# A two-block transformer kernel: the buffers of the split weights start at 0x00 instead of 0xC0 of each 256 bytes

## The chip, the cores and the metric

The kernel runs on one core of one Trainium2 chip. The metric is the device time of one execution in microseconds. It was taken three times for the kernel before; the median is quoted, and one further execution was recorded by the hardware profiler.

## The reference, cut to what matters

The reference is a stack of three kinds of layer on 512 latent rows of width 1024 (and 256 context rows): an FNet layer with a gated feed-forward (`swiglu`), a differential-attention layer with another `swiglu`, and then a hybrid layer (a Mamba-2 scan beside forgetting attention). Nearly all its arithmetic is dense products of activations with weight matrices that are used once:

```
x = x + g2 * swiglu(modulate(rms_norm(x, gain), sh2, sc2), ffn_w_in[i], ffn_w_out[i])   # i = 0 (lat and ctx), i = 1 (lat)
q, k, v = split(h @ diff_w_in, 3);   o = finish(attention(q, k, v)) @ diff_w_out
proj = rmsnorm(h) @ w_in_2           # z, x, B, C, dt, z_att, q, k, v, f, gates
merged = g_ssd * (y_ssd @ w_proj_ssd) + g_att * (y_att @ w_proj_att)
out = h + rmsnorm(merged @ w_out, norm_post)
```

Everything is float32. The kernel keeps that precision by splitting each float32 operand `a` into a rounded part `aH` and a remainder `aL`, both of type float32r, and by forming `a*w` as `aH*wH + aL*wH + aH*wL`.

## The kernel before, in words

**The stream.** SyncE loads the weights in blocks of 128 partitions x 8 x 256 floats (1 MB) in the order of `stream_plan` into a ring of two slots (`ring`, line 240). ScalarE copies a block into `wH` (lines 1833 and 1842) when TensorE has finished with the block two places earlier in the plan. VectorE writes `wL = ring - wH` (lines 2567 and 2578). TensorE then uses the block. `wH` and `wL` have two slots each (`NS = 2`), so one block is split while the other is used. The order of the blocks is written out by hand in `stream_plan`; nothing in it depends on an address.

**How a block is used.** In most products the 128x128 piece of `wH` or `wL` is the stationary operand, loaded by a weight load of its own, and the activations are the moving operand. In four places the activations are stationary and 256 columns of the weight block move: values of the attention (line 1053), the gate rows `z` of the scan (line 1352), the values of the second attention (line 1528) and the last product (line 1299). The helpers `tile` and `exact` (lines 689 and 694) do both feed-forwards. `gemm` (line 1287), `scan_unit` (lines 1333, 1352 and 1356), `narrow` (lines 1503 to 1547), `pair_gemm` (lines 1012 to 1035), `first_pair` (line 1064), `out_part` (line 1115) and `first_unit` (line 950) do the rest.

**Addresses.** `sb` hands out SBUF one buffer behind another, rounded up to 32 bytes, and `phase`/`leave` free what was handed out in a stage. `apart` makes the pair H and L. Empty buffers named `space...` move what follows. With the sizes in the code, the buffers that TensorE reads begin at these addresses modulo 256 (both of a pair alike, and all 128x128 pieces of `w`, all rows of `h1`, `hid`, `un`, `h2` and so on too, because their pitches are multiples of 256 bytes):

| buffer | start modulo 256 | where TensorE starts to read |
|---|---|---|
| `w` | 0xC0 | 0xC0 |
| `h1`, `hid` | 0xC0 | 512 latent columns at 0xC0, 256 context columns at 0x80 (`H1_CTX = LAT + 48`) |
| `h2`, `ao`, `mg` | 0x00 | 0x00 |
| `un` | 0xC0 | 512 columns from column 16: 0x00; the first 272 columns: 0xC0; the last 256: 0x00; as stationary operand 0x00 |
| `ys`, `ya` | 0xC0 | 0xC0 |
| `xs`, `df` (the Fourier transform over rows) | 0x40 | 0x40 |

**Counts.** From the loops, products with a float32r operand pair come in these numbers. Of 512 moving columns at 0xC0 with a piece of `w` stationary: in the feed-forwards 2 layers x 21 units x 48 = 2016 and 2 layers x 24 x 22 = 1056 at line 689 and 96 at line 950, `ys` 384, `ya` 192, together 3744. Of 512 moving columns at 0x00: 576 at line 1547, 192 at line 1287, 192 at line 1115, 144 each at lines 1023 and 1035, 96 at line 1064, together 1344. Of 256 moving columns at 0x80: 1536 at line 694. Of 256 at 0x00: 552 at line 1356, 192 at line 1510, 144 at line 1012, 48 at line 1064, together 936. Of 272 at 0xC0: 552 at line 1356 and 192 at line 1503, together 744. With 256 columns of `w` moving at 0xC0 and 128 stationary columns at 0x00: 768 at line 1352, 576 at line 1053, 384 each at lines 1299 and 1528, together 2112.

Of the kernel before, what the change touches and what calls it, by code (L numbers as in the profile page):

```python
# [12 lines left out]
P = 128  # L13
# [155 lines left out]
def bass_two_blocks_kernel(nc, io, kt_d, dl_d, dc_d, xsave, out):  # L169
# [36 lines left out]
    with ExitStack() as ctx:  # L206
        here = [ctx]

        def sb(name, shape, dt=F32):
            return here[-1].enter_context(nc.sbuf_tensor(name, shape, dt))  # L210
# [31 lines left out]
        def apart(name, shape):  # L242

            return sb(name + "H", shape, F32R), sb(name + "L", shape, F32R)


        def phase():
            s = ExitStack()
            here.append(s)
            return s  # L250

        def leave():
            here.pop().close()

        phase()
        early = sb("early", [P, 4, KC, 256])
        leave()
        wH, wL = apart("w", [P, NS, KC, 256])
        phase()
        xT = sb("xT", [P, KC, ROWS])  # L260
        adacc = sb("adacc", [P, 2, 2, 256])
        condz = sb("condz", [P, KC, 32])
# [51 lines left out]
        yold, xds, zA, gab = gap[:, 0, :], gap[:, 1, :], gap, gap  # L314
        ckT, cqT = sb("ckT", [16, ALL]), sb("cqT", [16, LAT])
        stt4 = sb("stt4", [P, 8])
        sb("space2", [P, 40])
        un = [t[:, :, 0:ALL] for t in apart("un", [P, KC, UN_PITCH])]
        phase()
        zrow = sb("zrow", [P, 4, 512])  # L320
# [56 lines left out]
        leave()  # L377
        leave()
        phase()
        under = sb("under", [P, 6168])  # L380
        orow = sb("orow", [P, 4, D])
        xback = sb("xback", [P, KC, LAT])
        oss, opre, ors = sb("oss", [P, 4, NT]), sb("opre", [P, NT]), sb("ors", [P, NT])
# [3033 lines left out]
```

## Time and profile before

| what | value |
|---|---|
| time, median of 3 runs | 2429.04 us |
| lowest, highest run | 2428.79 us, 2433.89 us |
| the profiled execution: its own time | 2427.2 us |
| the profiled execution: span from first to last instruction | 2425.0 us |
| mean granted TensorE clock | 0.999 |
| instructions | 34386 |

All durations that are used below come from the one profiled execution. Its own time is 2.2 us over its span, and 1.8 us under the median of the three runs. A matmul's duration in the profile is a modelled one: from its start to the moment at which its last column has left the array, so that consecutive matmuls overlap. What a matmul costs a busy TensorE is the distance from its start to the next start.

### The profile page before, as it was taken

How to read it: one execution, taken by the hardware profiler on the slowest of the kernel's cores; microseconds unless marked ns; L12 is line 12 of the kernel's file. 1: busy time of each engine (PE TensorE's matmuls, PEld its weight loads, DVE VectorE, ACT ScalarE, POOL GpSimd, SP SyncE). 2: the span in 40 equal slices, each digit the busy share in tenths (PEclk: the TensorE clock that was granted, in tenths of full speed). 3: DMA queues.
4: the chain of work that ended last, by engine and by line, in shares of the span. 5: the costliest groups of instructions: out<-in, count | busy, mean ns of one | idle time of the engine just before them, and what ended most of it. 6: DMA issues, size and time to landing. Idle time of an engine off the chain costs nothing.

```text
span 2425.0 us, 34386 instructions
## 1 busy us (share of the span) xinstructions
PE 2356.3 (97%) x14108; PEld 1975.3 (81%) x14108; DVE 1367.6 (56%) x2269; ACT 879.5 (36%) x1499; POOL 374.4 (15%) x301
## 2 busy tenths in 40 slices
PE   7899999999999999999999999999999999999999
PEld 5678888888878777657888887988989878887788
DVE  3775766666546767775333336365566445555433
ACT  4332111211234544444222224464545334444432
POOL 0210000000015434501000001143343410000000
PEclk9999999999999999999999999999999999999999
DMA  9834344344321111112333323212222122112223
GB/s 320 218 102 123 122 125 123 121 136 119 94 83 35 36 53 36 36 52 70 104 87 104 90 89 100 71 53 70 70 70 70 53 78 62 54 58 65 85 90 113
DMA packets 252743, 220.76 MB, mean 91 GB/s; under 512 B 7480, under 2 KB 243443, under 8 KB 252204
## 3 DMA queue, kind: packets, MB, share of 16 engines
q1 hardware_dynamic: 249072, 217.92, 29.5%
q8 instruction: 112, 1.84, 0.3%
q10 hardware_dynamic: 3260, 0.58, 0.1%
q14 instruction: 43, 0.35, 0.0%
q0 software_dynamic: 256, 0.07, 0.0%
HBM read 214.26 MB, written 6.29 MB: 91 GB/s over the span
## 4 chain that ended last, share of the span: by engine, by line
PE 60%; DVE 3%; ACT 2%; issue 1%; POOL 1%; DMA 0%; SPq 0%; DVEq 0%; ACTq 0%; POOLq 0%
PE two L689 11%; PE bank L1547 5%; PE bank L1356 5%; PE bank L689 4%; PE bank L1352 3%; PE bank L1333 3%; PE two L1287 3%; PE bank L1053 2%; PE bank L1528 2%; PE two L1567 2%; PE bank L1184 2%; PE two L1158 2%; PE bank L1023 1%; PE bank L1035 1%; PE two L1445 1%
## 5 line engine op out<-in xcount | busy, mean ns | idle before, releaser
L2578 DVE TENSOR_TENSOR wL<-ring,wH 128x512 fp32r<-128x512 f32 x224 | 180.1, 820 | 144.4 <-ACT wH L1842 144.2
L1833 ACT ACTIVATE wH<-ring 128x2048 fp32r<-128x2048 f32 (+1 forms) x80 | 149.2, 1865 | 260.7 <-PE bank L694 69.6
L2567 DVE TENSOR_TENSOR wL<-ring,wH 128x2048 fp32r<-128x2048 f32 (+1 forms) x80 | 180.0, 2250 | 80.1 <-ACT wH L1833 79.9
L689 PE MATMUL two<-h1H,wH 128*128 128x512 f32 x496 | 194.9, 393 | 0.0
L689 PE MATMUL two<-h1H,wL 128*128 128x512 f32 x496 | 193.1, 389 | 0.0
L689 PE MATMUL two<-h1L,wH 128*128 128x512 f32 x496 | 192.9, 389 | 0.0
L1842 ACT ACTIVATE wH<-ring 128x512 fp32r<-128x512 f32 x224 | 133.7, 623 | 57.6 <-PE bank L1333 20.5
L2482 DVE SCALAR_TENSOR_TENSOR adacc<-ring,cond,adacc 128x256 f32<-128x256 f32 x378 | 151.9, 479 | 0.0
L1912 ACT ACTIVATE gateS<-two 128x512 f32<-128x512 f32 x44 | 26.3, 598 | 316.9 <-PE bank L694 134.8
L1356 PE MATMUL bank<-unH,wH 128*128 128x272 f32 (+1 forms) x368 | 111.3, 302 | 3.9 <-ACT cin L2103 2.1
L689 PEld LDWEIGHTS two<-h1H,wL 128*128 128x128 f32 x496 | 93.1, 188 | 19.6
L689 PEld LDWEIGHTS two<-h1H,wH 128*128 128x128 f32 x496 | 93.2, 188 | 18.7 <-issue 0.4
L689 PEld LDWEIGHTS two<-h1L,wH 128*128 128x128 f32 x496 | 93.2, 188 | 18.2
L2671 DVE SCALAR_TENSOR_TENSOR xT<-two,ada,xT 128x512 f32<-128x512 f32 (+1 forms) x48 | 30.6, 680 | 135.7 <-PE bank L694 35.9
L1356 PE MATMUL bank<-unL,wH 128*128 128x272 f32 (+1 forms) x368 | 104.4, 284 | 0.0
L1356 PE MATMUL bank<-unH,wL 128*128 128x272 f32 (+1 forms) x368 | 104.3, 283 | 0.0
L689 PE MATMUL two<-hidH,wH 128*128 128x512 f32 x264 | 103.7, 393 | 0.2 <-DVE hidL L2702 0.2
L689 PE MATMUL two<-hidH,wL 128*128 128x512 f32 x264 | 102.8, 389 | 0.0
L689 PE MATMUL two<-hidL,wH 128*128 128x512 f32 x264 | 102.7, 389 | 0.0
L3214 POOL TENSOR_TENSOR rstd<-rstd,sq 128x768 f32<-128x768 f32 x5 | 11.6, 2329 | 559.2 <-ACT sq L1870 559.0
L1547 PE MATMUL bank<-unH,wH 128*128 128x512 f32 x192 | 86.9, 453 | 0.6 <-ACT lamv L2269 0.4
L2296 ACT ACTIVATE probA<-two,amx 128x144 f32<-128x144 f32 (+3 forms) x64 | 34.7, 542 | 144.8 <-DVE amx L3083 144.7
(650 smaller groups left out, 6918.5 us busy)
## 6 DMA issues: line engine op xcount, KB each, us to landing
ring<-in_ffn_w_in SPq DMA_DIRECT2D x88, 512.0 KB, 5.2
ring<-in_w_in SPq DMA_DIRECT2D x40, 1024.0 KB, 5.3
ring<-in_w_ada SPq DMA_DIRECT2D x32, 1024.0 KB, 5.3
ring<-in_ffn_w_out SPq DMA_DIRECT2D x16, 1024.0 KB, 5.2
early<-in_w_ada SPq DMA_DIRECT2D x12, 1024.0 KB, 12.2
ring<-in_diff_w_in SPq DMA_DIRECT2D x12, 1024.0 KB, 5.1
ring<-in_w_proj_ssd SPq DMA_DIRECT2D x8, 1024.0 KB, 5.1
ring<-in_ffn_w_out SPq DMA_DIRECT2D x8, 768.0 KB, 4.7
```

The costliest lines, as they stand in the source:

```text
L689: m = nc.tensor.matmul(bank[3 * s + half], w, r[:, 0:LAT], start=i == 0, stop=i == n - 1)
L1053: m = nc.tensor.matmul(bank[b][:, 256 * (i % 2):256 * (i % 2) + 256], h2[x][:, kc, i * P:(i + 1) * P], w[y][:, kc, :], start=k == 0, stop= ...
L1287: m = nc.tensor.matmul(o[:, at:at + hi - lo], w[y][:, kc, P * j:P * j + P], a[x][:, kc, lo:hi], start=k == 0, stop=k == 3 * KC - 1)
L1333: m = nc.tensor.matmul(bank[b], w[y][:, kc, P * t:P * t + P], ys[x][:, kc, :], start=k == 0, stop=k == 11)
L1352: m = nc.tensor.matmul(bank[b][:, 256 * (t % 2):256 * (t % 2) + 256], un[x][:, kc, META + P * t:META + P * t + P], w[y][:, kc, :], start=k ...
L1356: m = nc.tensor.matmul(bank[b][:, 0:hi - lo], w[y][:, kc, P * j:P * j + P], un[x][:, kc, lo:hi], start=k == 0, stop=k == 3 * KC - 1)
L1547: m = nc.tensor.matmul(bank[6 + j], w[y][:, kc, P * j:P * j + P], un[x][:, kc, META:ALL], start=k == 0, stop=k == 3 * KC - 1)
L1833: nc.scalar.activation(hi, raw, ACT.Copy).then_inc(w_hi, 1)
L1842: nc.scalar.activation(hi[:, 2 * r:2 * r + 2, :], raw[:, 2 * r:2 * r + 2, :], ACT.Copy, scale=colA[:, c:c + 1] if SPLIT[n][0] == "ps" else ...
L2482: m = nc.vector.scalar_tensor_tensor(out=o, in0=w[:, kc, :], scalar=x, in1=o, op0=ALU.mult, op1=ALU.add)
L2567: nc.vector.tensor_tensor(lo, raw, hi.bitcast(F32), ALU.subtract).then_inc(w_lo, 1)
L2578: nc.vector.tensor_tensor(lo, raw, hi.bitcast(F32), ALU.subtract).then_inc(q_lo, 1)
```

## The change

`wH` and `wL` move up by 64 bytes, so that they begin at 0x00 modulo 256. In the first block's stages a further 192 bytes follow them, so that everything behind them moves by 256 bytes and keeps its address modulo 256. In the second block's stages `space2` gives back 64 bytes and `under` too, so that `un` and all behind it, `orow` and `xback` keep their very addresses. Between the two, `acc`, `gap`, `ckT`, `cqT` and `stt4` (lines 312 to 316) stand directly behind `w` and in front of `space2`; they move by 64 bytes with `w`. `ring` and `early` stay where they are. No instruction is added, removed or reordered, and no wait changes.

```diff
         phase()
         early = sb("early", [P, 4, KC, 256])
         leave()
+        sb("space7", [P, 16])
         wH, wL = apart("w", [P, NS, KC, 256])
         phase()
+        sb("space8", [P, 48])
         xT = sb("xT", [P, KC, ROWS])
...
         stt4 = sb("stt4", [P, 8])
-        sb("space2", [P, 40])
+        sb("space2", [P, 24])
         un = [t[:, :, 0:ALL] for t in apart("un", [P, KC, UN_PITCH])]
...
-        under = sb("under", [P, 6168])
+        under = sb("under", [P, 6152])
         orow = sb("orow", [P, 4, D])
```

## Rows read from the trace of the kernel before

**Rows 1.** The page's first part: busy time, share of the span, instructions.
```profile
span 2425.0 us, 34386 instructions
PE 2356.3 (97%) x14108; PEld 1975.3 (81%) x14108; DVE 1367.6 (56%) x2269; ACT 879.5 (36%) x1499; POOL 374.4 (15%) x301
```

**Rows 2.** Busy time by stretch: both feed-forwards, and the late gate products.
```profile
core 0: us, PE busy (x) PEld busy (x) DVE busy (x) ACT busy (x) POOL busy (x), PEclk, DMA share, GB/s
160.00:690.00 530.00, 529.81 (x3119) 469.66 (x3118) 327.27 (x639) 101.99 (x108) 2.41 (x1) 1.00 0.38 116
1113.00:1480.00 367.00, 364.45 (x1598) 299.20 (x1599) 135.26 (x124) 102.10 (x110) 8.61 (x7) 1.00 0.33 96
2283.00:2380.00 97.00, 97.00 (x461) 81.24 (x461) 36.87 (x27) 29.02 (x24) 0.00 (x0) 1.00 0.28 88
```

**Rows 3.** Timeline of PE (start us, us, name): a tile of 24 matmuls, 512 columns.
```profile
1136.36 0.39 PE L689 MATMUL two<-h1H,wH 128*128 128x512 f32 x1
...
1141.80 0.39 PE L689 MATMUL two<-h1H,wH 128*128 128x512 f32 x1
```

**Rows 4.** Groups by form, PE (count | busy us, mean ns | idle): 512 columns at 0xC0.
```profile
L689 PE MATMUL two<-h1L,wH 128*128 128x512 f32 x496 | 192.9, 389 | 0.0
...
L689 PE MATMUL two<-hidL,wH 128*128 128x512 f32 x264 | 102.7, 389 | 0.0
...
L1333 PE MATMUL bank<-ysL,wH 128*128 128x512 f32 x128 | 50.2, 392 | 0.0
...
L1287 PE MATMUL two<-yaL,wH 128*128 128x512 f32 x32 | 12.5, 391 | 0.0
```

**Rows 5.** Timeline of PE: 24 matmuls of 512 columns at 0x00, and the next start.
```profile
2289.23 0.39 PE L1287 MATMUL two<-unH,wH 128*128 128x512 f32 x1
...
2294.73 0.39 PE L1287 MATMUL two<-yaH,wH 128*128 128x512 f32 x1
```

**Rows 6.** Groups by form, PE: 512 columns at 0x00, and last 0x40 with stationary 0x40.
```profile
L1547 PE MATMUL bank<-unL,wH 128*128 128x512 f32 x192 | 75.7, 394 | 0.0
...
L1287 PE MATMUL two<-unL,wH 128*128 128x512 f32 x64 | 25.1, 393 | 0.0
...
L1115 PE MATMUL bank<-aoL,wH 128*128 128x512 f32 x52 | 20.5, 395 | 0.0
...
L805 PE MATMUL two<-dfL,xsH 128*128 128x512 f32 x32 | 12.5, 391 | 0.0
```

**Rows 7.** Timeline of PE: 24 matmuls of 256 context columns, and the next start.
```profile
396.83 0.28 PE L694 MATMUL two<-h1H,wH 128*128 128x256 f32 x1
...
399.65 0.39 PE L689 MATMUL two<-h1H,wH 128*128 128x512 f32 x1
```

**Rows 8.** Timeline of PE: 46 distances between starts, 256 columns of `w` moving.
```profile
1555.03 0.28 PE L1352 MATMUL bank<-wL,unH 128*128 128x256 f32 x1
...
1560.25 0.28 PE L1352 MATMUL bank<-wH,unL 128*128 128x256 f32 x1
```

**Rows 9.** Groups by form, PE: products of 256 and 272 columns.
```profile
L1352 PE MATMUL bank<-wH,unL 128*128 128x256 f32 x256 | 71.2, 278 | 0.0
...
L1053 PE MATMUL bank<-wH,h2L 128*128 128x256 f32 x192 | 53.1, 277 | 0.0
...
L1356 PE MATMUL bank<-unL,wH 128*128 128x272 f32 x184 | 53.0, 288 | 0.0
...
L1356 PE MATMUL bank<-unL,wH 128*128 128x256 f32 x184 | 51.4, 279 | 0.0
...
L694 PE MATMUL bank<-h1L,wH 128*128 128x256 f32 x176 | 49.5, 281 | 0.0
...
L1299 PE MATMUL two<-wL,mgH 128*128 128x256 f32 x80 | 22.3, 279 | 0.0
...
L1528 PE MATMUL bank<-wL,unH 128*16 128x256 f32 x32 | 8.8, 276 | 0.0
```

## The prediction

> **What bounds the kernel.** I read the page's first part, then the busy time by stretch, then the groups by form and the timeline of TensorE. TensorE is busy for 2356.3 of 2425.0 us [rows 1]. In the two feed-forwards and the late gate products its busy time equals the stretch to within 1%, while VectorE is busy for 62%, 37% and 38% of it and ScalarE for less [rows 2]. So in these stretches a nanosecond more or less between two starts of matmuls lands in the time, and the splitting engines have room. In the two attention stages and in the scan TensorE also waits, and part of a change would vanish there; I count it in full and let the range carry that.
>
> The change has nothing in it but addresses. The question is whether the distance between two starts depends on where the operands lie. The trace answers in part, since it holds the same instruction at several addresses:
>
> - 512 columns moving from 0xC0, a piece of `w` at 0xC0 stationary: 24 starts take 1141.80 - 1136.36 = 5.44 us, 226.7 ns each [rows 3].
> - 512 columns moving from 0x00, `w` at 0xC0: 24 starts take 2294.73 - 2289.23 = 5.50 us, 229.2 ns each, 2.5 ns more [rows 5]. Both stretches are unbroken, on the same array, with the same shapes and no wait inside.
> - 256 columns from 0x80, `w` at 0xC0: 24 starts take 399.65 - 396.83 = 2.82 us, 117.5 ns [rows 7].
> - 256 columns of `w` moving from 0xC0, stationary operand at 0x00: 46 starts take 1560.25 - 1555.03 = 5.22 us, 113.5 ns [rows 8]. Per column that is 0.443 ns, as in the 226.7 ns of the first case, so 0.443 ns a column looks like the floor, and 4.0 to 4.2 ns a matmul are lost in the third case.
>
> The modelled duration shows the same: a matmul of 512 columns at the floor lasts 389 ns, one of 256 lasts 276 ns, and the mean of a group is higher by what its members lose. `h1` and `hid` show 389 [rows 4]; `un` and `ao`, read from 0x00, show 393 to 395 [rows 6]. The 256 columns at 0x80 and 0x00 show 281 and 279, those of moving `w` 277 to 279 [rows 9]. So the position matters by 1% to 4% of a matmul. What the trace does not show is the pair that the change makes: `w` stationary at 0x00.
>
> **The change, part by part.**
>
> *512 columns at 0xC0, 3744 matmuls.* The operands begin alike now, and with `w` at 0x00 they no longer do. I take it that the floor belongs to pairs that begin alike. For it: the one pair alike at another place, `df` and `xs` at 0x40, has 391 [rows 6], nearer 389 than the 393 to 395 of the unlike pairs. Against it: `ys` is alike too and has 392 [rows 4], though its tiles are short and start after waits. Price: 2.5 ns, that of the nearest unlike pair in an unbroken stretch [rows 5], so 3744 x 2.5 = +9.4 us. The bounds: 0 (the position of `w` does not matter), and 6 ns, that of the worst unlike group (395 - 389, [rows 6]), so +22.5 us. Below nothing it can't go, since `h1` and `hid` are at the floor.
>
> *512 columns at 0x00, 1344 matmuls.* These pairs become alike. Price by the same step: -2.5 ns, -3.4 us. Bounds: 0, and the whole 4 to 6 ns that these groups lose now, -5 to -8 us.
>
> *256 columns at 0x80 and at 0x00, 1536 + 936 matmuls.* They lose 4.0 ns or so now [rows 7, 9]. The first stay unlike, the second become alike. No full row shows a pair of 256 columns alike with 128 stationary ones. I take 0. Bounds: all of the loss goes, 2472 x 4.0 = -9.9 us; or they get worse by as much as they lose now, +9.9 us.
>
> *272 columns at 0xC0, 744 matmuls.* They last 288 ns against 276 + 16 x 0.443 = 283 at the floor [rows 9], although the operands begin alike. I take 0, with -3.7 and +3.7 us as bounds.
>
> *`w` moving, 2112 matmuls.* The moving start goes from 0xC0 to 0x00, the stationary operand stays at 0x00. The means of 277 to 279 against 276 [rows 9] say that a fifth to a half of them are slow now. I take 0. Bounds: all reach the floor, 2112 x 2 = -4.2 us; all become slow, 2112 x 3 = +6.3 us.
>
> *What else moves.* ScalarE writes `wH` and VectorE reads and writes at the new addresses; if a split took a few per cent longer, the room of rows 2 hides it. If that room were gone, each block would show as a wait of TensorE. `acc` and `gap` move by 64 bytes; they are elementwise operands of VectorE and ScalarE, and `gap` enters fewer than fifty products. Nothing. The transfers into `ring` keep their addresses. No queue, wait or issue is moved.
>
> The sum is 9.4 - 3.4 = +6.0 us. It is made against the profiled execution, 2425.0 us of span and 2427.2 us in all, and carries over to the median of 2429.04 us, 1.8 us above it: **2435.0 us**.
>
> **Where the skill speaks against it.** Rows 3 and 5 differ by 2.5 ns a matmul with nothing changed but the start. The Trainium skill, page SBUF — State Buffer, section "Who interferes with whom", gives TensorE two independent read ports, one for the moving operand and one for weight loads, and says that TensorE never waits on anyone; the same page's 16-byte lines would treat 0xC0 and 0x00 alike. By that page every term above is 0. The trace does not agree with it for the moving start, and has no row for the stationary one.
>
> **The rivals.**
>
> *Nothing measurable changes (0.25).* The stationary piece is read ahead into the array during the matmul before, which at 512 columns leaves it time; its start may not count, and what rows 3 and 5 show would be the moving start alone. For it: the groups differ by their moving operand in all my 512-column rows, as `w` is always at 0xC0 there. Then only `w` moving and the 256s could change, and both signs are open: 2429, within 5 us.
>
> *The moving start alone decides (0.12).* 0xC0 is cheap and 0x00 and 0x80 dear. For it: 16 stationary columns with `w` moving at 0xC0 show 276 [rows 9]. Against it: the 272 columns start at 0xC0 and lose 5 ns. Then only the 2112 products with moving `w` become slow, up to +6.3 us: 2435.
>
> *The stationary start decides where the matmul is short (0.20), the other side.* At 256 columns a weight load has hardly more time than it needs. All full weight loads from 0xC0 in front of 256 or 272 columns go with a loss, and the one combination at the floor has its stationary operand at 0x00 [rows 7 to 9]. With `w` at 0x00 the 2472 matmuls gain 4.0 ns and the 744 gain 5, so -9.9 - 3.7 = -13.6 us, while the 512s stay: **2415.4 us**. It decides as soon as the 256s gain more than 2.4 ns each, since 2472 x 2.4 covers the 6.0 us of my sum. Against it: more than half of the 256s with stationary `mg` at 0x00 are slow all the same (279, [rows 9]).
>
> *Both mechanisms (0.13).* -13.6 + 6.0 = -7.6 us: 2421.4.
>
> **How the numbers follow.** My forecast, the alike pair, has 0.30. A measurement of this kernel can tell about 0.2%, 4.9 us, from no change. Slower by more: the forecast and the moving-start rival, 0.42. Within: 0.25. Faster: the stationary start alone or with the forecast, 0.33. The range runs from 2415, where the faster rival lies, to 2446, which takes the 512s at 5 ns instead of 2.5 and some of the 256s with it. The cases are of both signs; the forecast's own range is 2430 to 2446.
>
> **What would show it.** Right: the feed-forward tiles of 24 take 5.50 us or more instead of 5.44 and their groups show over 391 instead of 389, while `un` and `ao` go from 393 to 395 down to 389 to 391. The stationary-start rival shows as 2.72 us instead of 2.82 for 24 matmuls of line 694. The moving-start rival shows as 281 at lines 1053, 1352 and 1299. If all groups keep their means within 1 ns, the change does nothing. I am wrong if the feed-forward tiles stay at 5.44 us.

## The result: 1.25% slower, and the profile after

| what | before | after |
|---|---|---|
| time, median of 4 runs each, taken side by side | 2431.03 us | 2459.98 us |
| lowest, highest | 2428.79, 2433.89 | 2458.37, 2461.08 |
| ratio, with 95% interval | | 1.0125 [1.0111, 1.0139] |
| span of the profiled execution | 2425.0 us | 2456.3 us |

I had written 2435.0 with a range of 2415 to 2446. The direction was right, the size was not: the time lies outside the range.

The page's first part for the changed kernel, against [rows 1]:

```profile
span 2456.3 us, 34386 instructions
PE 2391.2 (97%) x14108; PEld 1988.5 (81%) x14108; DVE 1362.3 (55%) x2269; ACT 880.6 (36%) x1499; POOL 375.9 (15%) x301
```

The span is 31.3 us longer, and TensorE is busy for 34.9 us more with the same 14108 matmuls. VectorE and ScalarE are busy for as long as before (1362.3 against 1367.6 us, 880.6 against 879.5 us), so the new addresses cost them nothing that shows. Busy time by stretch, for the same three stages as in [rows 2] (columns: us, then busy us and instructions of PE, PEld, DVE, ACT, POOL, then PEclk, DMA share, GB/s):

```profile
162.00:699.00 537.00, 536.90 (x3100) 467.80 (x3099) 324.54 (x634) 100.52 (x106) 2.41 (x1) 1.00 0.37 114
1127.00:1498.00 371.00, 370.84 (x1587) 297.83 (x1588) 131.29 (x119) 97.49 (x103) 8.28 (x5) 1.00 0.31 91
2313.00:2411.00 98.00, 98.00 (x466) 81.53 (x465) 36.86 (x27) 29.07 (x24) 0.00 (x0) 1.00 0.28 91
```

TensorE is still the only engine that fills these stages, at a granted clock of 1.00. The added time is no wait. It is in the distance from one matmul's start to the next. The timeline of TensorE in the changed kernel (start us, us, name), first and last row of each of the four stretches that answer to [rows 3, 5, 7 and 8]:

```profile
1149.92 0.40 PE L691 MATMUL two<-h1H,wH 128*128 128x512 f32 x1
...
1155.52 0.40 PE L691 MATMUL two<-h1H,wH 128*128 128x512 f32 x1
...
2318.56 0.39 PE L1289 MATMUL two<-unH,wH 128*128 128x512 f32 x1
...
2324.00 0.39 PE L1289 MATMUL two<-yaH,wH 128*128 128x512 f32 x1
...
402.17 0.28 PE L696 MATMUL two<-h1H,wH 128*128 128x256 f32 x1
...
405.03 0.40 PE L691 MATMUL two<-h1H,wH 128*128 128x512 f32 x1
...
1577.50 0.28 PE L1354 MATMUL bank<-wL,unH 128*128 128x256 f32 x1
...
1583.01 0.28 PE L1354 MATMUL bank<-wH,unL 128*128 128x256 f32 x1
```

- 512 columns at 0xC0, `w` at 0x00: 24 starts take 5.60 us, 233.3 ns each. It was 226.7.
- 512 columns at 0x00, `w` at 0x00: 24 starts take 5.44 us, 226.7 ns. It was 229.2.
- 256 columns at 0x80, `w` at 0x00: 24 starts take 2.86 us, 119.2 ns. It was 117.5.
- 256 columns of `w` moving from 0x00, stationary at 0x00: 46 distances take 5.51 us, 119.8 ns. It was 113.5.

The groups by form say the same for the whole kernel (count | busy us, mean ns of one | idle), to be read against [rows 4, 6 and 9]; an operation's line is two higher than before:

```profile
L691 PE MATMUL two<-h1L,wH 128*128 128x512 f32 x496 | 196.0, 395 | 0.0
...
L691 PE MATMUL two<-hidL,wH 128*128 128x512 f32 x264 | 104.3, 395 | 0.0
...
L1549 PE MATMUL bank<-unL,wH 128*128 128x512 f32 x192 | 75.5, 393 | 0.0
...
L1354 PE MATMUL bank<-wH,unL 128*128 128x256 f32 x256 | 72.3, 283 | 0.0
...
L1055 PE MATMUL bank<-wH,h2L 128*128 128x256 f32 x192 | 54.3, 283 | 0.0
...
L1358 PE MATMUL bank<-unL,wH 128*128 128x272 f32 x184 | 52.8, 287 | 0.0
...
L1358 PE MATMUL bank<-unL,wH 128*128 128x256 f32 x184 | 52.0, 282 | 0.0
...
L1335 PE MATMUL bank<-ysL,wH 128*128 128x512 f32 x128 | 50.5, 395 | 0.0
...
L1289 PE MATMUL two<-unL,wH 128*128 128x512 f32 x64 | 24.9, 389 | 0.0
...
L1117 PE MATMUL bank<-aoL,wH 128*128 128x512 f32 x52 | 20.4, 393 | 0.0
```

`h1`, `hid` and `ys` went from 389 to 392 up to 395. `un` at the gates fell from 393 to 389, but `un` at line 1549 only from 394 to 393 and `ao` from 395 to 393. The products with `w` moving went from 277 and 278 to 283 at lines 1055 and 1354.

Both kernels issue the same matmuls in the same order, so the k-th start of one can be subtracted from the k-th start of the other. That shows where along the span the 31.2 us between the last starts come from:

| matmul number | start before, us | later after the change, us | what lies between |
|---|---|---|---|
| 1200 | 199.8 | +1.4 | Fourier layer and beginning |
| 4000 | 675.5 | +10.9 | first feed-forward |
| 6400 | 1150.2 | +14.0 | differential attention |
| 8000 | 1504.5 | +23.6 | second feed-forward |
| 13200 | 2265.2 | +29.5 | scan and second attention |
| last | 2419.7 | +31.2 | gates and last product |

In the feed-forwards the time is added evenly: 2.67 us per 400 matmuls in the second, which is 6.7 ns for each, and 1.38 us per 400 in the first, where only half have 512 columns.

### The profile page after: what moved, and what is told of

Same layout as the page of the kernel before. It is cut to its first block, busy times and chain, and to the rows that moved or that the text cites. A ratio compares the mean times of both kernels' runs of the same rounds, so it can differ in the third digit from the quotient of the medians.

```text
span 2456.3 us, 34386 instructions
## 1 busy us (share of the span) xinstructions
PE 2391.2 (97%) x14108; PEld 1988.5 (81%) x14108; DVE 1362.3 (55%) x2269; ACT 880.6 (36%) x1499; POOL 375.9 (15%) x301
## 4 chain that ended last, share of the span: by engine, by line
PE 89%; DVE 4%; ACT 3%; DMA 2%; issue 2%; POOL 0%; SPq 0%; ACTq 0%; DVEq 0%; POOLq 0%
PE two L691 22%; PE bank L691 8%; PE bank L1549 5%; PE bank L1358 4%; PE bank L696 4%; PE two L696 4%; PE bank L1354 4%; PE bank L1335 3%; PE bank L1055 3%; PE two L1289 3%; PE bank L1530 2%; PE two L1569 2%; PE bank L1186 2%; PE two L1160 2%; PE bank L1037 1%
## 5 line engine op out<-in xcount | busy, mean ns | idle before, releaser
L1358 PE MATMUL bank<-unH,wH 128*128 128x272 f32 (+1 forms) x368 | 111.7, 303 | 3.9 <-ACT cin L2105 2.1
```

The lines of the kernel that those rows point to most:

```text
L1358: m = nc.tensor.matmul(bank[b][:, 0:hi - lo], w[y][:, kc, P * j:P * j + P], un[x][:, kc, lo:hi], start=k == 0, stop=k == 3 * KC - 1)
```

## The experiments

A distance is from one start to the next, and a loss is the distance less the floor of 0.443 ns per column (226.7 ns for 512, 113.3 ns for 256, 120.4 ns for 272). The losses are means over all neighbouring float32r matmuls of equal width whose distance is within 25 ns of the floor, some 9,750 in each trace. d is the start of the stationary operand less the start of the moving one, modulo 256 bytes; a pair with d = 0 is called alike. The kernel before is 21.7 us over the floor by this count, and the changed one 54.9 us. The difference, 33.2 us, is near the 31.3 us of the span; the rest may be absorbed by waits, which was not shown.

Four kernels moved `w` alone or with its neighbours, run beside the kernel before (median 2428.72 us).

**The distance kept, everything moved by 64 bytes.** `space7` without `space8` and without the smaller `space2`: `w` and nearly all behind it move together. To make room, `xm` lies over a buffer that is free by then.

```diff
+        sb("space7", [P, 16])
         wH, wL = apart("w", [P, NS, KC, 256])
...
-        xm = sb("xm", [P, 4, META])
+        xm = ada[1][:].rearrange("p a b -> p (a b)")[:, 0:4 * META].rearrange("p (a n) -> p a n", a=4)
```

> The split weights and every buffer behind them move by 64 bytes together, so each pair of TensorE operands keeps its distance modulo 256 while all absolute positions change (one small buffer, xm, is laid over a dead one to make room). Theory 1, the distance between the two operands decides: the time stays within 5 us of the kernel before (2426 to 2436), a feed-forward tile of 24 matmuls of 512 columns takes 5.44 us. Theory 2, the absolute start of the weights at 0x00 is the dear one: as slow as the changed kernel, 2455 to 2465, the tile takes 5.60 us.

Measured: 2431.62 us, ratio 1.0008 [0.9997, 1.0019]. Its feed-forward group is at the floor, with `w` and `h1` both at 0x00:

```profile
L690 PE MATMUL two<-h1L,wH 128*128 128x512 f32 x496 | 193.1, 389 | 0.0
```

The very `w` at 0x00 that costs 29 us in the changed kernel costs next to nothing when its partners move along. The absolute start of `w` decides nothing of the size in question. The place is not quite without effect: the products with `w` moving lose 2.6 ns instead of 1.5 at the same distance.

**`w` moved by 256 bytes.** `space7` of 64 elements, `xm` as above, and `under` smaller by 64 elements.

> The split weights move by 256 bytes, to 0xC0 again, all else as before modulo 256 (xm laid over a dead buffer). Both theories: no change, 2426 to 2436, tile of 24 at 5.44 us. Slower than that would mean that the move itself, or acc and gap moving with it, costs something.

Measured: 2428.21 us, 0.9995 [0.9984, 1.0005]. So a move of `w` by a whole 256 bytes costs nothing.

**`w` at 0x40 and at 0x80.** The same edit as the change, with 32 and 48 elements in `space7` and the other empty buffers sized to match (for 0x80 `xm` is laid over the free buffer too).

> The split weights at 0x40, everything else at its old address modulo 256. Theory 1 (distance): 3744 matmuls of 512 columns at 0xC0 get the distance +0x80, which no row shows yet; 1344 of 512 columns at 0x00 get the distance that costs 6.7 ns in the changed kernel (+4.4 us against before); the 2112 with moving weights get the distance -0x40 that costs 4.3 ns (+5 us). With 0 to 7 ns for the first group: 2440 to 2466. Theory 2 (absolute start): anything, since no row has weights at 0x40; the groups of 512 columns at 0xC0 and at 0x00 would show the same loss, while by theory 1 those at 0x00 show 6.7 ns.

> The split weights at 0x80 (xm laid over a dead buffer). Theory 1 (distance): 3744 matmuls of 512 columns at 0xC0 get the distance -0x40, which costs 2.3 to 2.5 ns in the kernel before (+9 us); 1536 context matmuls of 256 columns at 0x80 become alike and cost 6.7 ns instead of 4.4 (+3.5 us); those with moving weights get 0x80. About 2440 to 2452. Theory 2: no forecast; it would show one loss for all groups with these weights stationary.

Measured: 2454.30 us (1.0104 [1.0078, 1.0129]) and 2448.38 us (1.0077 [1.0060, 1.0094]). Groups by form of the kernel with `w` at 0x80:

```profile
L691 PE MATMUL two<-h1L,wH 128*128 128x512 f32 x496 | 194.7, 393 | 0.0
...
L696 PE MATMUL two<-h1L,wH 128*128 128x256 f32 x160 | 45.2, 283 | 0.0
```

The second row tells most. `w` and the 256 context columns both start at 0x80 there, and 283 is 2 ns above the 281 of [rows 9], where they were 64 bytes apart. At 256 columns the alike pair is the dearer one.

Four more kernels, beside the kernel before at 2428.06 us.

**The changed kernel with `h1` and `hid` at 0x00 too.**

```diff
+        sb("space9", [P, 16])
         h1 = apart("h1", [P, KC, PITCH])
```

> The changed kernel with the feed-forward operands h1 and hid moved by 64 bytes as well, so that they are alike with the weights again; nothing else is different. If the distance decides, 3072 matmuls of 512 columns get back 6.6 ns each (20 us) and the context columns go from distance 0x80 to +0x40 (1 us): about 2439, and 24 matmuls of line 691 take 5.44 us again. If something else in the move makes the kernel slower (the splitting engines, the moved acc and gap), it stays above 2450.

Measured: 2439.33 us, 1.0046 [1.0031, 1.0061]. Its groups by form:

```profile
L692 PE MATMUL two<-h1L,wH 128*128 128x512 f32 x496 | 193.1, 389 | 0.0
...
L1336 PE MATMUL bank<-ysL,wH 128*128 128x512 f32 x128 | 50.6, 395 | 0.0
```

The feed-forward is back at 389 with `w` still at 0x00, and `ys`, left at 0xC0, stays at 395. The kernel is 11.3 us over the kernel before beside it, where the changed one was 29.0 us over its own. So nearly 18 us of the loss came from the feed-forwards, nearly all of it from their unlike pairs of 512 columns (the context columns, now at d = 0x40, gain 0.9 ns each), and most of what is left are the other 256s.

**The changed kernel with `wH` back at 0xC0, so that `wL` alone is at 0x00.** A product's own pair and the weight load that runs beside it (the next product's) now differ in their distance.

```diff
-        wH, wL = apart("w", [P, NS, KC, 256])
+        wH = sb("wH", [P, NS, KC, 256], F32R)
+        sb("space7", [P, 16])
+        wL = sb("wL", [P, NS, KC, 256], F32R)
```

> Only the low halves wL move to 0x00, wH stays at 0xC0. In the feed-forwards TensorE repeats three products: wH with aH, wH with aL, wL with aH. Theory A, the loss comes from the moving operand and the weight load that runs beside it (that of the next product): the product of wH with aL is the one that is followed by a late start. Theory B, it comes from the product's own two operands: that of wL with aH is. In both a third of the 512-column products lose up to 6.7 ns: 8 us, with moving wL another 3 us: 2436 to 2444.

Measured: 2450.64 us, 1.0093 [1.0078, 1.0108], slower than the 2436 to 2444 that I expected. Timeline of TensorE in its second feed-forward:

```profile
1300.35 0.40 PE L692 MATMUL bank<-h1H,wL 128*128 128x512 f32 x1
1300.59 0.39 PE L692 MATMUL bank<-h1H,wH 128*128 128x512 f32 x1
1300.81 0.39 PE L692 MATMUL bank<-h1L,wH 128*128 128x512 f32 x1
1301.04 0.40 PE L692 MATMUL bank<-h1H,wL 128*128 128x512 f32 x1
```

Over all of these products at line 692 the next start comes 235 ns after one with `wL`, 228.7 after `h1H,wH` and 229.4 after `h1L,wH`, during which the load of `wL` runs. The 235 sits at the product whose own operands are unlike, not at the one beside whose load the distance is unlike. That speaks for the own pair. But the two alike products lose 2.0 and 2.7 ns as well, and the time is well above the third of the loss that the own pair alone would give. So a product's start-to-start time also depends on the pairs beside it. How, stays open.

**`w` 32 bytes further, at 0xE0.**

> The split weights move by 32 bytes, to 0xE0, all else as before modulo 256. If only whole steps of 64 bytes count, the time stays within 5 us of the kernel before. If the loss grows with the distance at any scale, about half of the changed kernel's: 2440 to 2450.

Measured: 2461.74 us, 1.0140 [1.0123, 1.0157], at least as much as 64 bytes, so neither of the two cases that I had written. The 512s at 0xC0 lose 6.5 ns.

**Bursts.** Behind the last result 24 matmuls in a row for each placement, reading `mg`, with nothing else to do. The diff shows one placement; the others differ in the offsets and in the number of stationary columns.

```diff
+            for n in (512, 384, 256, 128):
+                for i in range(24):
+                    nc.tensor.matmul(bank[6][0:128, 0:n], ml[:, 0 + P * i:0 + P * i + 128], mh[:, 48 + P * i:48 + P * i + n], start=True, stop=True)
...
```

> The kernel before with bursts of 24 equal products after its last result (they add nothing to the outputs and some 0.2 ms to the span), from a clean start, moving from mgH and stationary from mgL: the four distances with 512, 384, 256 and 128 columns, the same distance at other absolute places, distances of 16 and 32 bytes, and stationary operands of 64 and 32 columns. By distance: 512 columns cost 226.7 ns at distance 0, 233 at +0x40, 232 at 0x80, 229 at -0x40; 256 columns 120 at 0, 113.3 or 117.7 at +0x40, 118.5 at 0x80, 117.7 at -0x40. If the loss is the moving stream and the weight load in each other's way, it shrinks with 64 and 32 stationary columns; if it is an offset of the product's start, it stays.

Measured (the kernel takes 2577.88 us with them), in groups by form:

```profile
L1717 PE MATMUL bank<-mgH,mgL 128*128 128x512 f32 x24 | 5.8, 396 | 0.0
...
L1723 PE MATMUL bank<-mgH,mgL 128*128 128x512 f32 x24 | 5.7, 394 | 0.0
...
L1714 PE MATMUL bank<-mgH,mgL 128*128 128x512 f32 x24 | 5.6, 389 | 0.0
...
L1714 PE MATMUL bank<-mgH,mgL 128*128 128x256 f32 x24 | 3.0, 282 | 0.0
...
L1717 PE MATMUL bank<-mgH,mgL 128*128 128x256 f32 x24 | 3.0, 281 | 0.0
...
L1729 PE MATMUL bank<-mgH,mgL 128*128 128x256 f32 x24 | 2.9, 276 | 0.0
L1750 PE MATMUL bank<-mgH,mgL 128*32 128x256 f32 x24 | 2.9, 276 | 0.0
```

Line 1714 is the alike pair, 1717 has the moving operand at 0xC0 and the stationary one at 0x00 (d = 0x40), 1723 has d = 0xC0, 1729 d = 0x40 with the operands at 0x00 and 0x40, and 1750 the alike pair with 32 stationary columns. The mean distance of the last 12 starts of a burst, in ns:

| | d = 0 | 0x40 | 0x80 | 0xC0 |
|---|---|---|---|---|
| 512 columns | 226.7 | 233.3 | 231.7 | 228.8 |
| 384 | 173.3 | 176.7 | 175.8 | 173.3 |
| 256 | 119.9 | 117.8 or 113.3 | 118.8 | 117.8 |
| 128 | 111.7 | 111.7 | 111.7 | 111.5 |

The effect needs nothing of this kernel's order or waits; while the bursts run, VectorE, ScalarE and GpSimd have no instruction. With 32 stationary columns the distance makes no difference: 231.7 ns at d = 0 and at d = 0x40 for 512 columns, 113.3 at both for 256. Whether the weight load and the moving stream get in each other's way is left open by this. At 256 columns the loss goes when the load is shorter, as it would by that explanation. At 512 columns it does not go: the alike pair gets dearer (226.7, then 230.0 and 231.7 ns with 64 and 32 stationary columns), and d = 0x40 only falls from 233.3 to 231.7. A stationary start 16 bytes on gives 233.3 already. At 128 columns the distance makes no difference either: 111.7 ns, against 56.7 at 0.443 ns a column, so something else bounds there. What, was not tested.

Three last kernels, beside the kernel before at 2428.51 us, for the part that I had not expected: dear alike pairs at 256 columns.

**The kernel before with `h2` at 0xC0.**

```diff
+        sb("space9", [P, 48])
         h2 = apart("h2", [P, KC, ROWS])
```

> The kernel before with one change: h2 (the operand of the second layer's projections) begins at 0xC0 instead of 0x00 modulo 256; w stays at 0xC0. In the 576 products of line 1053, where 256 columns of w move and h2 is stationary, both now begin alike. Theory A (the distance between the own moving and stationary start decides, and at 256 columns the alike pair is the worst): starts at line 1053 go from about 114 to about 120 ns apart, +3.0 us; the 336 products of 512 columns of h2 (lines 1023, 1035, 1064) become alike and lose their 3.5 ns, -1.1 us; the 192 of 256 columns get 2 ns worse, +0.4 us; in sum +2.3 us over the kernel before. Theory B (the absolute moving start decides): line 1053 keeps 114 ns, the 512s at 0xC0 go to the floor, -1.1 us. Theory C (alike is good at every width, as I wrote blind): line 1053 goes to 113.3 ns, and the sum is about -2.5 us.

Measured: 2431.71 us, 1.0012 [1.0004, 1.0021]. Timeline of TensorE in it, 24 starts with the stationary operand alike:

```profile
759.27 0.28 PE L1054 MATMUL bank<-wH,h2H 128*128 128x256 f32 x1
...
762.15 0.28 PE L1054 MATMUL bank<-wH,h2H 128*128 128x256 f32 x1
```

That is 120.0 ns where the kernel before has 113.8 at these products. `w` did not move at all. The other part of expectation A failed: the 512-column products of `h2`, alike now, lose 3.8 ns instead of 3.0, where I had them gain 3.5. What holds them back is said below the last table.

**The kernel before with its context columns alike.**

```diff
-PITCH, H1_CTX, HID_CTX, UN_PITCH = 832, LAT + 48, LAT + 48, 576
+PITCH, H1_CTX, HID_CTX, UN_PITCH = 832, LAT, LAT, 576
```

> The kernel before with one change: the context columns of h1 and hid stand directly behind the 512 latent ones, so that the 1536 products of 256 columns at the line of the context (694 in the kernel before) start at 0xC0, as their piece of w does, instead of 0x80. Theory A (at 256 columns the alike pair is the worst): 24 starts take 2.88 us (120 ns each) instead of 2.82, +2.9 us over the kernel before. Theory B (only w moving is hurt by being alike): 117.7 ns as before, no change. Theory C (alike is good at every width): 2.72 us, -6.7 us.

Measured: 2433.40 us, 1.0017 [1.0007, 1.0026]. The tile of 24 context products in its timeline, to compare with [rows 7]:

```profile
399.16 0.28 PE L694 MATMUL two<-h1H,wH 128*128 128x256 f32 x1
...
402.03 0.40 PE L689 MATMUL two<-h1H,wH 128*128 128x512 f32 x1
```

2.87 us, 119.6 ns each instead of 117.5. Both runs say that at 256 columns the alike pair is the worst one, whichever operand is `w`.

**The changed kernel with `h2` at 0x40.**

```diff
+        sb("space9", [P, 16])
         h2 = apart("h2", [P, KC, ROWS])
```

> The changed kernel (w at 0x00) with one more change: h2 begins at 0x40 instead of 0x00. Theory A (the distance decides, wherever the pair stands): the 576 products of line 1055, now with the stationary operand 64 bytes behind the moving one as in the kernel before, return from about 119.7 to about 115 ns between starts, -2.6 us; the 336 products of 512 columns of h2 at 0x40 with w at 0x00 stay within 1 ns, +0.3 us at most; the 192 of 256 columns gain, -0.5 us; in sum 2 to 3 us less than the changed kernel, 2457. Theory B (w moving from 0x00 is slow because of its own start): line 1055 stays at 119.7 ns and the time at 2460.

Measured: 2459.68 us, 1.0123 [1.0105, 1.0141]. By the distances the expectation holds: the sum over the floor is 52.0 us instead of 54.9, the distance at this line is 114.8 ns instead of 119.8, and the group is at 278 instead of 283:

```profile
L1056 PE MATMUL bank<-wH,h2L 128*128 128x256 f32 x192 | 53.3, 278 | 0.0
```

By the time it is not to be seen: the interval is about 4 us wide to either side. The profiled execution was even 5.5 us longer than that of the changed kernel. Its granted clock was 0.91 on the mean of its first 100 us, against 0.98 in the changed kernel:

```profile
0.00:100.00 100.00, 81.41 (x614) 55.84 (x615) 47.67 (x122) 36.10 (x71) 2.64 (x7) 0.91 0.97 296
```

Its 1200th matmul starts 5.3 us later than in the changed kernel, before `h2` is used at all. This run bears the rule of distances out and says nothing on the time.

**All together.** Mean loss per matmul over the floor, ns, with d behind it; the last two columns are the whole loss and the span, us:

| kernel | 512, `h1 hid ys ya` | 512, `un h2 ao` | 256, context | 256, `w` moving | 256, `un h2` | loss | span |
|---|---|---|---|---|---|---|---|
| before | 0.3 (0) | 3.5 (C0) | 4.4 (40) | 1.5 (40) | 4.3 (C0) | 21.7 | 2425.0 |
| `w` + 256 bytes | 0.4 (0) | 3.3 (C0) | 4.5 (40) | 1.7 (40) | 4.3 (C0) | 22.1 | 2425.9 |
| all + 64 bytes | 0.7 (0) | 3.3 (C0) | 4.4 (40) | 2.6 (40) | 3.6 (C0) | 24.3 | 2427.1 |
| changed | 6.6 (40) | 2.9 (0) | 5.3 (80) | 6.4 (0) | 6.2 (0) | 54.9 | 2456.3 |
| `w` at 0x40 | 5.8 (80) | 6.5 (40) | 4.5 (C0) | 4.2 (C0) | 1.8 (40) | 48.5 | 2449.9 |
| `w` at 0x80 | 2.7 (C0) | 5.6 (80) | 6.4 (0) | 5.4 (80) | 5.2 (80) | 44.6 | 2446.2 |
| `w` at 0xE0 | 6.5 (20) | 6.3 (E0) | 4.4 (60) | 5.0 (20) | 3.7 (E0) | 53.4 | 2459.9 |

One distance gives nearly one loss in columns that share neither buffer nor line: at 512 columns d = 0x40 gives 6.5 to 6.6, 0x80 gives 5.6 to 5.8, 0xC0 gives 2.7 to 3.5. At 256, d = 0 gives 6.2 to 6.4, 0x80 gives 5.2 to 5.4. Two things don't fit the rule: `un`, `h2` and `ao` alike lose 2.9 on the mean, and d = 0x40 at 256 columns gives either 1.5 to 2.6 or 4.4.

The starts in the traces explain the first. These products come in short pieces between other work, `un` at line 1549 in pieces of six. In the changed kernel the first three distances of a piece lose 5.3 ns for `un`, 5.5 for `ao` and 5.9 for `h2`; the later ones lose 0.5, 0.8 and 1.5. (Distances more than 25 ns over the floor, such as the one just behind other work, stay out.) In the kernel before, where d is 0xC0, `un` loses 4.8 and then 2.1. `h1`, alike there, loses 1.8 in the first three and 0.0 from the fourth on. So an alike pair of 512 columns reaches its floor only after some three products without a break, and short pieces gain little from being alike. Why the second differs stays open.

No placement tried beats the kernel before. It has the alike pair at most of its 512s and d = 0x40 where `w` moves. The 272s, not in the table, lose 5.1 ns alike, 3.4 at d = 0x40, and 6.2 and 6.0 at 0x80 and 0xC0.

## Why the prediction was wrong in size

**What bounds the kernel, and that the pair decides at 512 columns: right.** The feed-forward tile takes 5.60 us, over the 5.50 that I had asked for, with 395 instead of 389, and no stall, wait or splitting engine has a part in it. The forecast's mechanism, that a pair of 512 columns is at the floor when it begins alike, is shown by the kernel with everything moved, by the one with `h1` moved back, and by the bursts. My second sign came true in part only: `un` went to 389 at the gates, but line 1549 and `ao` stayed at 393.

**512 columns at 0xC0: the step that failed first.** I wrote "Price: 2.5 ns, that of the nearest unlike pair in an unbroken stretch", +9.4 us. Measured are 6.6 - 0.3 = 6.3 ns over all of them, and 3744 x 6.3 = +23.6 us. The row that I took the price from has d = 0xC0; the change makes d = 0x40. I had treated all unlike pairs as one case. The upper bound, 6 ns and +22.5 us, was nearly the value, but by chance: it was read off `ao`, whose d was 0xC0 as well. And I ended the range at 5 ns.

**`w` moving: the second step that failed.** I took 0 with +6.3 us as the bound. Measured are 6.4 - 1.5 = 4.9 ns, and 2112 x 4.9 = +10.3 us, over the bound. I had carried the 512s' rule over as a possible gain, while at 256 columns the alike pair is the worst of the multiples of 64 bytes. Two sets of rows of the kernel before had hinted that alike is not the floor there. The 272 columns start alike and lose 5 ns [rows 9], which I noted and then priced at nothing. And the products of `xs` and `df` with 256 columns, alike at 0x40, lose 5.3 ns in the trace before, which I had not looked up.

**512 columns at 0x00.** I took -3.4 us. Measured is 3.5 to 2.9, -0.6 ns, and 1344 x 0.6 = -0.8 us. The 2.5 ns came back in full at the gates (229.2 to 226.7), where the products follow each other without a break, and hardly at line 1549, where they come in pieces of six and 255 of the 408 distances that count are among the first three of a piece. I had priced short pieces like an unbroken stretch.

**The other 256s and the 272s.** I took 0 for each. Measured: context 0.9 ns x 1536 = +1.4 us, `un` and `h2` 1.9 ns x 936 = +1.8 us, 272 columns 3.4 instead of 5.1, 744 x 1.7 = -1.3 us. All are inside my bounds.

**The sum.** 23.6 + 10.3 - 0.8 + 1.4 + 1.8 - 1.3 = 35.0 us against 31.3 us of span. I had said that a part would vanish in stages where TensorE also waits; that the 3.7 us did so was not measured by itself.

**The rivals.** That nothing changes fell with the first tile. The Trainium skill, page SBUF — State Buffer, section "Who interferes with whom", says that TensorE's moving operand and its weight loads have read ports of their own and that TensorE waits on no one. The bursts don't fit that: with the same instructions and no other engine's work beside them, the start of the moving operand alone makes 226.7 or 233.3 ns, and with 32 stationary columns it makes no difference. That the moving start alone decides had its sign met, 281 or more where `w` moves (283), but it falls with the kernel that moved everything (512 columns moving from 0x00, stationary at 0x00 too, 0.7 ns) beside `w` at 0x40 (moving from 0x00, stationary at 0x40, 6.5 ns). That the stationary start decides where the matmul is short falls with the context tile, which went from 117.5 to 119.2 ns, and not to 113.3, and the case of both mechanisms falls with it.

**The range.** With my own bounds the slow side reached 22.5 + 6.3 + 9.9 + 3.7 = 42.4 us above the time before. It was cut to 2446 by mixing middling values of terms that all hang on one unknown, the loss by distance, and so don't average out.

## What to carry to other kernels

Where TensorE is the bound and matmul follows matmul, the start of the stationary operand relative to the moving one, modulo 256 bytes, is worth up to 6.7 ns a matmul: 3% at 512 columns and close to 6% at 256. In this kernel, float32r pairs of 512 columns were cheapest at the same start modulo 256, once three or more ran without a break. Pairs of 256 columns were dearest there, and a stationary start 64 bytes behind the moving one was the best or within about a nanosecond of it. A new buffer that looks harmless in front of one of them can undo it. When a price is read off rows for an effect with a hidden variable, look for the row with the same value of that variable (here the distance), and set the range by moving all its terms together.

## What was unexpected of the hardware

- A stationary start 16 bytes on already costs in full at 512 columns (233.3 ns, bursts), and 32 bytes did in the whole kernel (1.0140). The place within 64 bytes counts too.
- The order turns over with the width: alike is best at 512 (226.7) and worst at 256 (119.9). At 384 columns d = 0 and d = 0xC0 are equal (173.3).
- At 256 columns and d = 0x40 a burst runs steadily at 117.8 ns with the operands at 0xC0 and 0x00, and steadily at 113.3 ns with 0x00 and 0x40. The absolute place does not select it: the products of line 1053, at 0xC0 and 0x00 too, run at 113.3 ns in long runs of the kernel before. What does is open. The context products of this kernel are in the slow one, and all of them in the fast one would save 1536 x 4.4 ns = 6.7 us, by estimate.
- Fewer stationary columns don't help at 512: with 64 of them the alike pair takes 230.0 ns, with 32 of them 231.7, both more than the 226.7 of 128 (one execution of the bursts).
